# Stick-breaking attention: the weights' multiplication moved from GpSimd to VectorE, the scores' lead shortened from two steps to one

## The reference, cut to what matters

```python
def _stick_breaking(q, k, v):
    _, _, s, d = q.shape
    scale = d ** -0.5
    for blk in range(s // SB_BLOCK):            # SB_BLOCK = 128
        q0 = blk * SB_BLOCK
        end = q0 + SB_BLOCK
        z = jnp.einsum('bhqd,bhkd->bhqk', q[:, :, q0:end], k[:, :, :end]) * scale
        mask = kj < qi
        log_keep = jnp.where(mask, jax.nn.log_sigmoid(-z), 0.0)
        rest = lax.cumsum(log_keep, axis=3, reverse=True) - log_keep
        a = jnp.where(mask, jnp.exp(jax.nn.log_sigmoid(z) + rest), 0.0)
        outs.append(jnp.einsum('bhqk,bhkd->bhqd', a, v[:, :, :end]))
```

## Time and profile before

| what | value |
|---|---|
| median of 3 runs | 3084.91 us |
| the profiled execution's own time | 3084.91 us |
| its span on the core | 3083.1 us |
| PE busy over the span | 2943.3 us, 95% |
| DVE, ACT, POOL busy | 49%, 25%, 36% |
| first sigmoid of the stage to the first matmul after it | 2739.81 to 2896.51 us |

### The profile page before, as it was taken

How to read it: one execution, slowest core, us unless ns; L and a number is a source line. 1 busy time by engine, 2 the same in 40 slices (tenths; PEclk the granted TensorE clock), 3 DMA queues, 4 the chain that set the end, 5 groups by cost and what they waited for, 6 DMA issues and landing times. The chain is left out here.

```text
span 3083.1 us, 48885 instructions
## 1 busy us (share of the span) xinstructions
PE 2943.3 (95%) x20526; PEld 2336.3 (76%) x20526; DVE 1508.3 (49%) x1499; ACT 769.0 (25%) x1106; POOL 1124.6 (36%) x627
## 2 busy tenths in 40 slices
PE   7998888999999989999999999999999899989999
PEld 6776777778878766788888888777887677866677
DVE  6454432324465343751614335667587433357561
ACT  5432222321011022200100001234233332257410
POOL 1331112444344412444444444412121353435552
PEclk9999899999999999999999999999999999999999
DMA  6243442442051201111111111122233533321143
GB/s 211 76 137 109 97 93 71 131 122 75 21 163 48 61 21 41 42 52 43 49 47 48 48 48 48 35 62 83 89 109 91 163 105 119 116 92 63 53 143 123
DMA packets 324857, 258.08 MB, mean 84 GB/s; under 512 B 46690, under 2 KB 285465, under 8 KB 324682
## 3 DMA queue, kind: packets, MB, share of 16 engines
q1 hardware_dynamic: 324426, 255.47, 27.8%
q10 hardware_dynamic: 256, 0.07, 0.0%
HBM read 192.05 MB, written 63.31 MB: 83 GB/s over the span
## 5 line engine op out<-in xcount | busy, mean ns | idle before, releaser
L160 POOL TENSOR_TENSOR w_hi<-w_raw,ones 128x1024 fp32r<-128x1024 f32 x162 | 392.3, 2421 | 1087.5 <-PE ps L279 796.5
L279 PE MATMUL ps<-h_hi,w_hi 128*128 128x512 f32 x2096 | 670.5, 401 | 7.1 <-POOL w_lo L176 3.7
L279 PE MATMUL ps<-h_lo,w_hi 128*128 128x512 f32 x2096 | 647.9, 390 | 0.0
L279 PE MATMUL ps<-h_hi,w_lo 128*128 128x512 f32 x2096 | 647.6, 390 | 0.0
L279 PEld LDWEIGHTS ps<-h_hi,w_hi 128*128 128x128 f32 x2096 | 392.7, 189 | 119.4 <-issue 36.3
L279 PEld LDWEIGHTS ps<-h_lo,w_hi 128*128 128x128 f32 x2096 | 394.6, 188 | 83.7
L279 PEld LDWEIGHTS ps<-h_hi,w_lo 128*128 128x128 f32 x2096 | 394.6, 188 | 83.1
L163 POOL TENSOR_TENSOR w_lo<-w_raw,w_hi 128x1024 fp32r<-128x1024 f32 x162 | 426.3, 2631 | 12.7
L176 POOL TENSOR_TENSOR w_lo<-w_raw,w_hi 128x1024 fp32r<-128x1024 f32 x30 | 73.1, 2438 | 304.9 <-ACT w_hi L171 304.9
L736 ACT CAST hid_hi<-w_raw 128x512 f32 (+1 forms) x64 | 39.7, 621 | 574.1 <-DVE w_raw L764 574.1
L279 PE MATMUL ps<-branch_hi,w_hi 128*128 128x512 f32 x512 | 162.1, 397 | 6.8 <-DVE mix_gate_b L2262 1.6
(11 more groups left out here) (506 smaller groups left out, 4204.8 us busy)
## 6 DMA issues: line engine op xcount, KB each, us to landing
w_raw<-in_w_in_dram SPq DMA_DIRECT2D x91, 512.0 KB, 4.9
w_raw<-in_w_up_dram SPq DMA_DIRECT2D x32, 512.0 KB, 4.0
w_raw<-in_w_down_dram SPq DMA_DIRECT2D x32, 512.0 KB, 3.6
kv_raw<-in_w_kv_dram SPq DMA_DIRECT2D x16, 512.0 KB, 5.2
mix_gates<-mix_sig SPq DMA_DIRECT2D x16, 512.0 KB, 3.0
mix_gate_b<-mix_gates SPq DMA_DIRECT2D x32, 256.0 KB, 4.2
mix_gates<-w_raw SPq DMA_DIRECT2D x16, 512.0 KB, 2.8
x_in<-in_x_dram SPq DMA_DIRECT2D x8, 512.0 KB, 9.1
```

Of the source, the lines that this page charges most:

```text
L160: pool.tensor_tensor(c.w_hi[:, s], c.w_raw[:, s], c.ones[:].unsqueeze(1).broadcast_to([P, KT, P]), ALU.mult).then_inc(c.w_rounded, 1)
L279: last = pe.matmul(o, w[:, s, k], a[:, k - offset, (half + h) * width:(half + h + 1) * width], start=(k == kts[0] and w is c.w_hi and a is ...
```

## The change

`weight` goes from four buffers to two, and a new tile `keep` of two buffers takes sigmoid(-z), which before overwrote the scores in PSUM. ACT now makes `keep` first and `weight` second. DVE scans from `keep`, waits for its own scans, and then does one multiplication over both heads at once; POOL does no more multiplications. The scores and sigmoids run one step ahead instead of two. The transposes of a step wait for the whole multiplication instead of for one head at a time. The semaphore `scanned` is gone.

```diff
-    weight = buf("weight", [P, 4, 2, HALF])
-    weight_t = buf("weight_t", [P, 2, 2, HALF])
+    keep, weight, weight_t = (buf(n, [P, 2, 2, HALF]) for n in ("keep", "weight", "weight_t"))
...
-            for n, (ct, qb, kh, width, diagonal) in enumerate(steps):
-                pool.wait_ge(kept, 2 * n + 1)
-                for hd in heads:
-                    pool.wait_ge(scanned, 2 * n + hd + 1)
-                    pool.tensor_tensor(weight[:, n % 4, hd, 0:width], weight[:, n % 4, hd, 0:width],
-                                       left[:, n % 2, hd, 1:width + 1], ALU.mult).then_inc(weighted, 1)
+            pool.wait_ge(weighted, n_steps)
             following.split_some(pool, 2)
...
-                wait(pe, scanned, 2 * (n - 1))
+                wait(pe, kept, 2 * (n - 1))
...
+                pe.wait_ge(weighted, n + 1)
 
                 wait(pe, copied, n)
                 for hd in heads:
-                    pe.wait_ge(weighted, 2 * n + hd + 1)
                     for t in range(width // P):
                         cut = slice(t * P, (t + 1) * P)
-                        last = pe.transpose(ps[:, 4 + hd, cut], weight[:, n % 4, hd, cut], c.ident[:])
+                        last = pe.transpose(ps[:, 4 + hd, cut], weight[:, n % 2, hd, cut], c.ident[:])
...
-            score(1)
             for n in range(n_steps):
-                if n + 2 < n_steps:
-                    score(n + 2)
+                if n + 1 < n_steps:
+                    score(n + 1)
...
-                wait(act, turned, n - 3)
+                wait(act, turned, n - 1)
                 z = ps[:, 2 * (n % 2):2 * (n % 2) + 2, 0:width]
-                act.activation(weight[:, n % 4, :, 0:width], z, ACT.Sigmoid).then_inc(kept, 1)
-                act.wait_ge(kept, 2 * n + 1)
-                act.activation(z, z, ACT.Sigmoid, scale=-1.0).then_inc(kept, 1)
+                act.activation(keep[:, n % 2, :, 0:width], z, ACT.Sigmoid, scale=-1.0).then_inc(kept, 1)
+                act.activation(weight[:, n % 2, :, 0:width], z, ACT.Sigmoid).then_inc(kept, 1)
...
-            sigmoids(1)
             for n, (ct, qb, kh, width, diagonal) in enumerate(steps):
-                if n + 2 < n_steps:
-                    sigmoids(n + 2)
+                if n + 1 < n_steps:
+                    sigmoids(n + 1)
...
-                wait(dve, weighted, 2 * (n - 1))
-                if not diagonal:
-                    dve.wait_ge(scanned, 2 * n)
                 if diagonal:
                     v.mark(dve.memset(l[:, :, width:width + 1], 1.0))
                 else:
                     v.mark(dve.tensor_copy(l[:, :, width:width + 1], left[:, (n - 1) % 2, :, 0:1]))
                 v.wait(dve)
+                dve.wait_ge(kept, 2 * n + 1)
+                for hd in heads:
+                    v.mark(dve.tensor_tensor_scan(l[:, hd, 0:width][:, ::-1], keep[:, n % 2, hd, 0:width][:, ::-1],
+                                                  c.ones[:, 0:1].broadcast_to([P, width]), l[:, hd, width:width + 1],
+                                                  ALU.mult, ALU.mult))
+                v.wait(dve)
                 dve.wait_ge(kept, 2 * n + 2)
-                for hd in heads:
-                    dve.tensor_tensor_scan(l[:, hd, 0:width][:, ::-1], ps[:, 2 * (n % 2) + hd, 0:width][:, ::-1],
-                                           c.ones[:, 0:1].broadcast_to([P, width]), l[:, hd, width:width + 1],
-                                           ALU.mult, ALU.mult).then_inc(scanned, 1)
+                dve.tensor_tensor(weight[:, n % 2, :, 0:width], weight[:, n % 2, :, 0:width], l[:, :, 1:width + 1],
+                                  ALU.mult).then_inc(weighted, 1)
+
+                dve.wait_ge(weighted, n + 1)
```

More of the change, by code:

```diff
@@ L4239, in stick_breaking @@
     loaded = inputs.loaded
-    made, scored, kept, scanned, weighted = (c.sem(f"sb_{n}") for n in ("made", "scored", "kept", "scanned", "weighted"))
+    made, scored, kept, weighted = (c.sem(f"sb_{n}") for n in ("made", "scored", "kept", "weighted"))
     turned, copied, summed = (c.sem(f"sb_{n}") for n in ("turned", "copied", "summed"))
@@ L4364, in before @@
                     pe.wait_ge(split[h], k - CT + 1)
-            pe.wait_ge(scanned, 2 * n_steps)
+            pe.wait_ge(kept, 2 * n_steps)
             following.multiply_early(pe, [([ps[:, 0], ps[:, 1]], range(CT)), ([ps[:, 2], ps[:, 3]], range(CT, KT))],
```

## The result

The changed kernel takes 3113.12 us (median of four runs, 3110.11 to 3115.34), the kernel before, run beside it, 3086.35 (3084.0 to 3088.9). The ratio is 1.0082, with a 95% interval of 1.0067 to 1.0096: slower by 21 to 30 us. The forecast was 3107.5 in a range of 3097 to 3118.

The account below looks back on a forecast made before the run. PE bounds the kernel now; after the change DVE's work plus waits for `keep` take 43.64 us a tile, four tiles less 0.6 giving 173.9, so +22.6 us on 3084.91: 3107.5 us, range 3097 to 3118.

Parts of the forecast that it names:

- DVE's work: DVE's scans, multiplication, memsets, copies and takes: 3.88 us a full step, 40.4 us a channel tile.
- 0.02 us off each: Possible gain per scan from reading `keep` in SBUF instead of PSUM; taken as nothing, about 1 us in all.
- the 65 ns a scan: Estimated SBUF-against-PSUM difference per scan from the Trainium skill's fixed cycles: some 3 us off the forecast, not counted.
- The lead: With one step of lead, product to scan two steps on takes 3.53 us, 4.17 with mask; 3.2 us of waits a tile.
- rival B: PE's granted clock falls once or twice per tile in its gaps, each some 3 us: 3120 to 3131 us; 7%.
- the table: Forecast of a tile's 12 steps, numbered 0 to 11, with DVE free, `keep` there, scan start and product times; 43.64 us.
- Start and end: First scan 0.4 us earlier, 0.6 us off four tiles in all; POOL's split and PE behind the last product 4.9 us.
- A: DVE alone sets the stage's pace and waits vanish: +10.3 us, or +8 with shorter scans, about 3095 us; 12%.
- C: DVE's 1.22 us product replaces POOL's 2.20 and the copies' stall goes: stage loses up to 10 us, 3075 us; 3%.
- the copies' stall: DVE's small copies held up beside POOL's multiplications, 0.74 us instead of 0.16: 9 us less DVE work with POOL idle.
- D: Seams after waits of 0.1 to 0.2 us at 48 products, half showing: +3 to +8 us; within the forecast's 78%.

Follow-up runs that it names:

- the kernel with the filler: To the changed kernel, twelve PE transposes of the identity into unused columns added at step 5 of each tile, ahead of the wait for its product: 3109.49 us, ratio 1.0064.
- the filler at step 3: To the changed kernel, twelve PE transposes of the identity added at step 3 of each tile, leaving the gap at step 5: 3109.84 us, ratio 1.0078.
- the first of the two kernels: To the kernel before, scans read `keep` in SBUF, made first, three buffers; lead of two and product on POOL stay: 3095.93 us, ratio 1.0038.

## Why the prediction was right

**DVE's work.** Forecast 40.4 us a tile, 161.6 in all. Measured: 176.4 less the waits for `keep` behind the start, 25.3 - 5.9 = 19.4, is 157.0. So it was 4.6 us too high in all. The instructions themselves fit: product 1.225 (forecast 1.22), a pair of scans of 512 keys 2.46 (2.46), copies 0.166 (0.16). From step 1 of the third tile to step 1 of the fourth it is 44.28 us (2840.99 to 2885.27), less 4.69 of waits 39.6: so a whole tile was 0.8 too high. Some 0.5 of that are its two `take` and two `take_rest`, 2.5 us for 3.0, since each takes 0.69 and overlaps the next instruction by 0.05 to 0.08; the rest are gaps that I put too wide between the instructions. That makes 3.2 for four tiles. The other 1.4 us are, nearly all, the last half's `take` and `take_rest`: the forecast counted eight of each, and only seven lie ahead of the last product. The same subtraction gives 156.9 in the kernel with the filler and 156.5 with the other sigmoid first, so this base is stable and the rest is waits. Two small sums of the forecast are off by a factor of two: there are 96 scans, so 0.02 us off each would have been 1.9 us, not about 1, and the 65 ns a scan that it estimated would have been 6.2 us, not some 3. Neither entered the sum.

**The lead.** The chain of 3.53 us, from product to the scan two steps on, was right as a mechanism and nearly in its size: in the third tile it is 3.38 from the end of product 3 (2850.89) to the scan of step 5 (2854.27). Steps 1 and 2 wait 1.55 and 0.24 us behind the first tile, against 1.68 and 0.29; step 5 waits 1.69, 1.46, 1.09 and 1.09 against 1.00. Putting the lead back takes away the waits, the falls of the clock ahead of the last scan, and 17.3 us.

**The clock (mis-sized).** This is the one step of the forecast that failed: "Against: no gap here is that long" and the price "each costing some 3 us", in rival B with 7%, whose own sign, a clock below 1.00 behind the start, did come. The step-7 waits come to 1.90 + 1.72 + 1.81 + 1.86 = 7.3 us against 1.0 in the sum. The clock did fall, once in each tile. The gaps ahead of it, 1.80 us three times and 2.17 once, are about the 1.6 to 1.7 of the table; what was wrong is the judgement that such a gap is too short, made from one row of a longer one. But a fall costs only some 1.5 us, since of what it delays only the transposes and scores lie within the handover, and their lengthening (0.88 + 0.56 in the second tile) reaches DVE. With the filler, which removes the falls, 5.0 us of the stage go: 6.2 at step 7, less 1.2 that come back in longer waits at other steps, the most of it in the first tile (1.12 at step 2, in place of 0.36 at step 3).

So the sum was 161.6 + 12.3 = 173.9, and what came is 157.0 + 19.4 = 176.4: 4.6 us too much for DVE's work, 7.1 too little for waits, of which 6.3 stand at step 7, nearly all of them the clock's. Two errors in opposite directions: that the sum came within 2.5 us is luck, and the range held the result by more than the terms deserved. The median of 3113.12 is 5.6 above the forecast; 2.9 of that are the stage (+25.5 for +22.6), 1.4 the kernel before, whose median is 3086.35 in this comparison and was 3084.91 in the forecast, and 1.3 the part outside the stage.

**Start and end.** POOL's split and PE's next work follow 5.0 us behind the last product (2926.45 to 2931.45), forecast and before 4.9.

```profile
2926.53 2.35 POOL L160 TENSOR_TENSOR w_hi<-w_raw,ones 128x1024 fp32r<-128x1024 f32 x1 [181.94 <-DVE sb_weight L4430]
2931.45 0.70 PE L279 MATMUL ps<-branch_hi,w_hi 128*128 128x512 f32 x2 [1.67 <-POOL w_lo L163]
```

**The rivals.** A (DVE alone) fell: the waits are there, 19.4 us. What it described exists with a lead of two. C (the shorter multiplication decides) fell: a product of 1.22 is shorter than POOL's 2.20, but it stands in DVE's queue, and the copies' stall was slack. D (wider seams) fell too; the seams are narrower than counted. PE busy was forecast near 142 and is 148.1 in the stage; the difference is what ran at the fallen clock. The kernel with the filler and no falls has 148.1 too, of which 4 x 1.53 are the filler, so 142.0 without it.

## What to carry to other kernels

Where three engines are balanced, compare the moved instruction not with its duration on the old engine but with the new engine's step against the pace of the bound one: here 3.88 against 3.1, which goes with 8 us more in the kernel with the lead put back, although the product itself got shorter. With a lead of one step, write out the chain from the end of a step to the start of the step after next, and compare it step by step with the one step that lies beside it: short steps show the gap that an average hides. A gap that opens on PE may bring a lower clock with it, so ask what stands right behind the gap, and whether it lies in the chain.

## What the runs showed of the hardware that was not expected

**Scans from SBUF beside POOL's multiplication.** A scan with both inputs in SBUF took 1271 ns alone, 1530 and 1639 beside POOL, and POOL's multiplication 1698 and 1616 in place of 1090; with the scan's data in PSUM both kept their times (1270, 1094). `keep` in SBUF is worth having only because POOL is silent there.

The Trainium skill ("SBUF — State Buffer", on who interferes with whom) says that a VectorE instruction with two SBUF inputs contends with a GpSimd instruction that reads SBUF. These runs agree: one input moved to PSUM, and the contention is gone. The Trainium skill also says ("SBUF — State Buffer", on the two separate sides) that of two such instructions the one that starts first holds the ports that they share for its whole length, and the other fully blocks. The trace of the first of the two kernels agrees there too. Three of its rows, start, duration, engine:

```profile
2816.92 1.09 POOL L4284 TENSOR_TENSOR sb_weight<-sb_weight,sb_left 128x512 f32<-128x512 f32 x1
2817.02 2.07 DVE L4438 TENSOR_TENSOR_SCAN sb_left<-sb_keep,sb_left,ones 128x512 f32<-128x512 f32 x1
...
2819.23 1.92 POOL L4284 TENSOR_TENSOR sb_weight<-sb_weight,sb_left 128x512 f32<-128x512 f32 x1 [1.23 <-DVE sb_left L4438]
```

The scan began while POOL multiplied and ended 1.08 us after POOL's end at 2818.01. The later multiplication began during the next scan, which ended at 2820.27, and ended 0.88 after that. It is so throughout: of the 48 scans of 512 keys 25 began during a multiplication, with 0.15 to 0.99 us of it left, and ended 1.08 us after it (1.14 the three with 0.15 left); 43 of the 48 multiplications of 512 began during a scan, with 0.32 to 1.12 us of it left, and ended 0.88 to 0.89 after it. So the second waits out whatever is left of the first, and a scan that begins late in a multiplication loses little. In the kernel before no such waiting shows: its multiplications took 1.09 beside a scan as well.

**A fall of the clock after a short idle stretch.** In the changed kernel it came as PE's gaps of 1.80 to 2.17 us ended, lasted 3.4 us at the lower of the two levels (1.2 GHz in place of 2.4), and went back. With the filler, which leaves 0.71 us of that gap, it did not come in the stage. But the length of the last gap alone does not tell. With the filler at step 3, a gap of 1.89 us brought it in one tile and not in two others, and behind 2.26 us it lasted 6.8. In the kernel with the other sigmoid first, a gap of 2.71 us in the third tile was followed by transposes at full clock:

```profile
2862.91 1.09 PE L4319 MATMUL ps<-ident,sb_weight 128*128 128x128 f32 x8 [2.71 <-DVE sb_weight L4430]
```

There the clock stayed at 1.00 for another 8.9 us and fell at 2871.8, while PE worked, 0.9 us behind a gap of 2.07. With only the lead taken away the falls came 0.6 to 2.2 us behind gaps of 1.73, and with the lead put back the one fall came with no gap over 1.15 in the 9 us ahead of it. What decides is not shown. Windows of 1 us of the changed kernel show the fall in its second tile:

```profile
2812.00:2813.00 1.00, 0.00 (x0) 0.00 (x0) 0.96 (x2) 0.45 (x1) 0.00 (x0) 1.00 0.00 0
2813.00:2814.00 1.00, 0.14 (x1) 0.14 (x2) 0.97 (x2) 0.00 (x0) 0.00 (x0) 0.76 0.00 0
2814.00:2815.00 1.00, 1.00 (x6) 1.00 (x7) 0.95 (x3) 0.00 (x0) 0.00 (x0) 0.50 0.07 16
...
2816.00:2817.00 1.00, 1.00 (x4) 0.26 (x4) 0.86 (x2) 0.88 (x1) 0.00 (x0) 0.53 0.45 162
2817.00:2818.00 1.00, 1.00 (x14) 0.62 (x14) 0.00 (x0) 0.50 (x1) 0.00 (x0) 1.00 0.01 2
```

The fall lies within the gap: a mean of 0.76 from 2813 to 2814 is about half at each level, so it came near 2813.5, ahead of the first transpose at 2813.86, and the rise is between 2816 and 2817.
